# First modulation and projection by quarters of the features; two projection chunks as seven block products

## The chip, the cores and the metric

The kernel runs as one program on one core of a Trainium2 chip. The metric is the time of the whole program on the device in microseconds, the median of several runs. TensorE (PE) does matrix products and transposes into the eight banks of PSUM, VectorE (DVE), ScalarE (ACT) and GpSimd (POOL) do elementwise work, and SyncE (SP) issues nearly all transfers from memory in one queue.

## The reference, cut to what matters

All of it is float32, for 256 tokens of 1024 features. The part that is touched is the start of the first block:

```python
def first_block(x, c, ada_w, ada_b, ln1_g, ...):
    cond = jax.nn.silu(c)
    mod = (cond @ ada_w[l] + ada_b[l])[:, None, :]
    sh1, sc1, g1, sh2, sc2, g2 = jnp.split(mod, 6, axis=-1)
    h = rms_norm(x, ln1_g[l]) * (1.0 + sc1) + sh1
    x = x + g1 * hybrid_mixer(h, w_in[l], w_out[l], ...)   # starts with h @ w_in, 2840 columns
    h = rms_norm(x, ln2_g[l]) * (1.0 + sc2) + sh2
    return x + g2 * sparse_moe(h, ...)                      # 32 experts, top 4
```

The mixer cuts the 2840 columns of `h @ w_in` into queries, keys and values of two attention variants. One of them compresses its keys with a small network (`cmp_w1`, `cmp_w2`). A second block with 272 tokens follows.

## The kernel before, in words

Features lie on the 128 partitions, in eight chunks of 128. Every engine has a program of its own, written out in order, and waits on counting semaphores. The weights of the first block pass through a ring of four slots of 2 MB. The list `A_LOADS` gives their order, and `a_freed(n)` the semaphore value at which the load in the same slot, four places earlier in the list, has been used: SP waits for that before it issues load n+4, and everything behind it in the list waits too.

The head runs so. x is transposed on TensorE (L872), copied out and squared on ScalarE (L1753, L1763), summed over the features with a matrix of ones (L880), and its root and reciprocal taken (L1765, L2130). The first third of the modulation (shift and scale, 2048 columns) is a product of `cond` with four loads of 2 MB (`mod`): two halves of the rows for each of two halves of the features. One group of matmuls takes four column groups of TensorE's array at a time (L889). VectorE copies the result out, TensorE transposes it, and VectorE adds the bias and scales the chunks of h (L2106 to L2121).

The projection runs over six chunks of columns (five of 512, one of 280) and two halves of the tokens, twelve products v = 0 to 11. The first four are done in two halves of the features (L947 to L973), with the remaining modulation between them. Products 4 to 11 (L975, L1018) contract all eight feature chunks at once. In between, TensorE transposes keys and queries (L986 to L1006), and runs the compression network (L1008), whose weights are the load `cmp`.

The second third of the modulation is summed over the rows on VectorE, in four passes over four loads (`add_modulation`, L2146). A product with ones then finishes it (L913). The last third runs on TensorE in eight halves (L901): two before the attention scores, six among them. The scores start with `score(0)` (L1084, L1143). From there on, attention, output projection, experts and the second block follow. The second block already uses the form of seven products of quarter blocks (Strassen's, in Winograd's variant), and the change takes its tables `UP_PRODUCTS` and `UP_FREED` over. GpSimd is idle between building its constants at the start and the attention's scaling, apart from copies of keys (L714) and a memset.

Of the kernel before, what the change touches and what calls it, by code (L numbers as in the profile page):

```python
# [40 lines left out]
P = 128  # L41
# [124 lines left out]
FIRST_SUMS = (QKV_SETS + 1, QKV_SETS + 1 + 2 * UP_SETS)  # L166
# [8 lines left out]
def b_freed(n):  # L175
# [17 lines left out]
    return "chunk_done", first + 4 * (c + 1)  # L193

# [69 lines left out]
class Memory:  # L264


    def __init__(self, nc, ctx):
# [68 lines left out]
        early_all = a.at  # L336
        self.modacc = self.OT.rearrange("p c t -> p (c t)")
# [140 lines left out]
z_done in_first z_copied doubled heads_ssq heads_root heads_normed gates_ready  # L478
# [34 lines left out]
def program_sync(nc, sp, m, s, a):  # L513
# [5 lines left out]
    def source(kind, layer, c):  # L519
# [4 lines left out]
        if kind == "mod":  # L524
            src = a["ada_w"][0, D // 2 * (c % 2):D // 2 * (c % 2 + 1), :].rearrange("(k p) n -> p k n", p=P)
            at = 512 * (c // 2)
            return [(slice(0, P), 2048, 512, src[:, :, at + D * n:at + D * n + 512]) for n in range(2)]
        if kind == "in" and c < 2:
            src = a["w_in"][0, D // 2 * c:D // 2 * (c + 1), 0:D]
            return [(slice(0, P), 4096, D, src.rearrange("(k p) n -> p k n", p=P))]  # L530
# [49 lines left out]
    for n, load_of in enumerate(A_LOADS):  # L580
# [3 lines left out]
        if load_of == ("in", 0, 5):  # L584
# [6 lines left out]
        elif n == RING - 1:  # L591
# [77 lines left out]
def program_gpsimd(nc, pool, m, s, a):  # L669
# [45 lines left out]

    pool.wait_ge(s["doubled"], 3)
    for u in range(UNITS):
        if u == 8:
            pool.wait_ge(s["heads_normed"], 5)
            pool.wait_ge(s["mod_ready"], 3)  # L720
# [121 lines left out]
def program_tensor(nc, pe, m, s, a):  # L842
# [21 lines left out]

    pe.wait_ge(s["c_loaded"], 16)
    turn_params(bank(0), 0, C)
    pe.wait_ge(s["x_loaded"], 16)
# [15 lines left out]
    def first_modulation(part):  # L883

        h, rows = part // 2, part % 2
# [2139 lines left out]
```

## Time and profile before

| | us |
|---|---|
| median of 3 runs | 1790.54 (1788.81 to 1790.69) |
| the profiled execution | 1793.06, its span 1791.3 |
| TensorE busy in the span | 1720.4 |
| VectorE, ScalarE, GpSimd busy | 712.0, 264.5, 134.5 |
| first projection starts | 23.86 |
| first attention scores start | 125.69 |

A float32 product of 512 columns shows as two records of TensorE, so eight matmuls are sixteen records. The granted clock is 1.00 at full speed (2.4 GHz) and 0.50 at the lower level (1.2 GHz). A row of the chain of waits names what the end waited for at that time. A transfer in it means that nothing else could have gone on.

### The profile page before, as it was taken

To read this page: it belongs to the slowest core of one execution; us is meant where nothing else is said; L and a number is where in the kernel's file an instruction comes from. 1 tells how busy PE (TensorE), PEld (TensorE's weight loads), DVE (VectorE), ACT (ScalarE), POOL (GpSimd) and SP (SyncE) were. 2 spreads that over 40 slices of the span, in tenths; PEclk is the share of its full clock that TensorE was granted. 3 is DMA by queue.
4 is the path that set the end of the run, shared out by engine and by line. 5 is a ranking of instruction groups with operands and counts; after the bars stand their busy time and mean duration, and the time that the engine had idled before them with its cause. 6 is when DMAs were issued, how large, how long until landed. Compare 5 with 4: busy or idle time off the path is not lost.

```text
span 1791.3 us, 25208 instructions
## 1 busy us (share of the span) xinstructions
PE 1720.4 (96%) x10215; PEld 1058.6 (59%) x10216; DVE 712.0 (40%) x1295; ACT 264.5 (15%) x535; POOL 134.5 (8%) x188
## 2 busy tenths in 40 slices
PE   7999999999999999999999999999999999999998
PEld 4456643333333333333333333797999998899987
DVE  2555422122121121212212121666678545768743
ACT  1136211011010100101011010214111001511100
POOL 4006400000000000001000010200100000010000
PEclk9999999999999999999999999999999999999999
DMA  8988999969999999999999999751254443535440
GB/s 313 342 284 249 387 417 429 430 283 428 429 428 428 427 428 428 429 428 428 428 428 428 429 428 428 262 187 48 95 185 145 172 159 118 200 142 188 159 171 24
DMA packets 95507, 548.11 MB, mean 306 GB/s; under 512 B 6002, under 2 KB 9282, under 8 KB 68722
## 3 DMA queue, kind: packets, MB, share of 16 engines
q1 hardware_dynamic: 95298, 546.93, 75.9%
q8 instruction: 48, 0.79, 0.2%
q10 hardware_dynamic: 144, 0.26, 0.0%
q14 instruction: 17, 0.14, 0.0%
HBM read 546.12 MB, written 1.05 MB: 305 GB/s over the span
## 4 chain that ended last, share of the span: by engine, by line
PE 77%; DMA 20%; ACT 1%; issue 1%; POOL 0%; DVE 0%; SPq 0%; DVEq 0%; POOLq 0%; ACTq 0%
DMA ring<-in_exp_w 18%; PE ps L1322 18%; PE ps L1609 11%; PE ps L1353 8%; PE ps L1638 6%; PE ps L1679 5%; PE ps L1454 4%; PE ps L1380 3%; PE ps L981 2%; PE ps L1287 2%; PE ps L1274 2%; PE ps L954 2%; PE ps L1195 2%; PE ps L1708 2%; DMA ring<-in_w_in 1%; PE ps L1733 1%
## 5 line engine op out<-in xcount | busy, mean ns | idle before, releaser
L1322 PE MATMUL ps<-ring,sq 128*64 128x512 f32 x2112 | 464.4, 593 | 23.9 <-DMA ring<-in_exp_w 23.9
L1322 PEld LDWEIGHTS ps<-ring,sq 128*64 128x64 f32 x2112 | 146.9, 137 | 316.7 <-issue 264.3
L1353 PE MATMUL ps<-arena,sq 128*64 128x512 f32 x1056 | 233.9, 595 | 3.5
L2360 DVE TENSOR_SCALAR sq<-arena,rstd 128x64 f32<-128x64 f32 x68 | 19.5, 329 | 365.2 <-PE ps L1322 364.6
L1353 PEld LDWEIGHTS ps<-arena,sq 128*64 128x64 f32 x1056 | 75.3, 137 | 140.8 <-issue 140.5
L2433 DVE TENSOR_SCALAR hn<-ps 128x512 f32<-128x512 f32 x33 | 22.8, 691 | 318.4 <-PE ps L1322 318.4
L1860 ACT ACTIVATE sq<-hn 128x512 f32<-128x512 f32 x33 | 20.8, 629 | 527.8 <-DVE hn L2433 527.8
L1753 ACT ACTIVATE sq<-ps 128x512 f32<-128x512 f32 (+1 forms) x99 | 51.9, 524 | 308.7 <-PE ps L1353 212.2
L1609 PE MATMUL ps<-arena 128*128 128x136 f32 (+1 forms) x768 | 90.0, 277 | 0.0
L1609 PEld LDWEIGHTS ps<-arena 128*128 128x128 f32 x768 | 88.6, 191 | 0.0
L1753 ACT ACTIVATE arena<-ps 128x512 f32<-128x512 f32 (+4 forms) x69 | 33.8, 500 | 279.8 <-PE ps L1638 78.4
L2483 DVE TENSOR_TENSOR arena<-ring 128x1024 f32<-128x1024 f32 x37 | 45.7, 1234 | 65.2 <-PE ps L1638 33.5
L1287 PEld LDWEIGHTS ps<-sq 64*128 64x128 f32 x528 | 48.7, 186 | 32.7 <-issue 26.0
L1287 PE MATMUL ps<-sq 64*128 64x256 f32 x528 | 66.9, 390 | 0.8 <-ACT sq L1753 0.7
L798 POOL TENSOR_TENSOR sq<-sq 128x272 f32<-128x272 f32 (+1 forms) x28 | 28.6, 1022 | 497.4 <-ACT sq L1880 294.8
L1274 PE MATMUL ps<-arena,sq 128*64 128x512 f32 x272 | 64.1, 592 | 0.2 <-DVE arena L2362 0.2
L1638 PE MATMUL ps<-arena 128*128 128x136 f32 x512 | 61.9, 279 | 0.0
L782 POOL TENSOR_TENSOR arena<-arena 32x1 f32<-32x1 f32 x5 | 0.9, 183 | 808.9 <-PE ps L1322 808.9
L1609 PE MATMUL ps<-hn,ring 128*128 128x136 f32 (+1 forms) x512 | 60.9, 277 | 0.0
L1638 PEld LDWEIGHTS ps<-arena 128*128 128x128 f32 x512 | 60.5, 190 | 0.0
L1609 PEld LDWEIGHTS ps<-hn,ring 128*128 128x128 f32 x512 | 59.6, 191 | 0.1
L1679 PE MATMUL ps<-arena 128*128 128x256 f32 x256 | 57.9, 379 | 0.0
(437 smaller groups left out, 2254.0 us busy)
## 6 DMA issues: line engine op xcount, KB each, us to landing
ring<-in_exp_w SPq DMA_DIRECT2D x123, 2048.0 KB, 21.1
arena<-in_exp_w SPq DMA_DIRECT2D x68, 2048.0 KB, 19.4
ring<-in_mlp_w_up SPq DMA_DIRECT2D x16, 2048.0 KB, 7.5
ring<-in_mlp_w_down SPq DMA_DIRECT2D x16, 2048.0 KB, 7.8
ring<-in_ada_w SPq DMA_DIRECT2D x8, 2048.0 KB, 12.3
ring<-in_sb_w_qkv SPq DMA_DIRECT2D x6, 2048.0 KB, 14.7
ring<-in_w_in SPq DMA_DIRECT2D x5, 2048.0 KB, 12.3
ring<-in_ada_w SPq DMA_DIRECT2D x8, 1024.0 KB, 9.9
```

The lines of the kernel that those rows point to most:

```text
L954: last = mm(bank(v), m.hn[:, kk, META + P * t:META + P * t + P], wt[:, k, at:at + 512], start=(kk == 0), stop=(kk == C - 1))
L1274: last = mm(bank(0)[64 * h:64 * h + 64, :], m.sel[:, t, :], m.h2[:, t, 512 * h:512 * h + 512], start=(t == 0), stop=(t == 1))
L1287: return mm(m.token_sum(c), m.y[rows, P * (c % 4):P * (c % 4) + P], m.selz[rows, h, :], start=False, stop=stop, skip_group_check=True)
L1322: last = mm(bank(2 + part)[64 * h:64 * h + 64, :], lhs, w[:, k % 2, at:at + 512], start=False, stop=(k == C - 1))
L1353: last = mm(bank(3)[64 * h:64 * h + 64, :], m.aT[:, q, 64 * half:64 * half + 64], w[:, q, 512 * h:512 * h + 512], start=(half == 0 and q = ...
L1380: last = mm(bank(banks[q] if banks else b0 + q)[:, lo:TT], w[:, k, P * q:P * q + P], act[:, k, lo:TT], start=(n == 0), stop=(n == C - 1))
L1454: last = mm(bank(qkv_bank(n, j))[:, half * f:half * f + half], weights_of(weights, w, m.wsum[:, n % 2], k)[:, P * f:P * f + P], inputs_of( ...
L1609: last = mm(bank(set_bank(n, j))[:, half * f:half * f + half], weights_of(weights, w, m.wsum[:, n % 2], k)[:, P * f:P * f + P], inputs_of( ...
L1638: last = mm(bank(b)[:, half * f:half * f + half], weights_of(weights, w, m.wsum[:, n % 2], k)[:, P * f:P * f + P], hidden_of(tokens, 0, gr ...
L1679: last = mm(bank(b)[:, 0:256], hidden_of(tokens, 1, group, k), weights_of(weights, w, m.wsum[:, n % 2], k), start=(group == 0 and k == 0), ...
L1753: f(dst, src, ACT.Copy, scale=scale).then_inc(s[name], 1)
L2483: link(v.tensor_tensor(t1, w[:, 0, :, 1], w[:, 0, :, 0], ALU.subtract))
```

## The change

Order of loads: the modulation's first third comes as four quarters of the features (all rows, 2 MB each), and with each of them the matching quarter of the rows of `w_in` for the first three column chunks (1304 columns, 1.3 MB). Behind them come chunks 3, 4 and 5 of the projection and the second modulation group by turns. `cmp` goes ahead of that group's last load. The loads of the biases of the experts now stand behind `cmp` and not behind the last chunk.

Head: VectorE copies x out of PSUM, and ScalarE only squares it, with its table loaded ahead. The reciprocal is applied to quarters. Filler products of the identity with itself (`idle_turns`) stand at six places of TensorE's program. The first three column chunks (v = 0 to 5) run in quarters of the features, the next quarter's modulation between them.

Chunks 4 and 5 (1024 columns) become two sets of seven products, each of four matmuls with 256 columns, instead of two products of eight with 512 for each. GpSimd makes four sums of token blocks once and four sums of weight blocks for each set (128x1024). ScalarE copies each set's first product, and VectorE adds the others up (`z_put`). The products are spread over the same places among the transposes.

The second third's last load is used on TensorE, by eight matmuls more in `modulation_sum`, and VectorE has three passes in the place of four. This sum and its transposes move behind the products. Semaphore counts of later users are shifted. The diff, cut to its core:

```diff
-A_LOADS = ([("mod", 0, 0), ("mod", 0, 1), ("in", 0, 0), ("mod", 0, 2), ("mod", 0, 3)]
-           + [("in", 0, 1), ("in", 0, 2), ("ada", 1, 0), ("ada", 1, 1), ("in", 0, 3), ("ada", 1, 2), ("in", 0, 4),
-              ("ada", 1, 3), ("in", 0, 5), ("cmp", 0, 0)] + [("ada", 2, k) for k in range(4)] + [("wout", 0, h) for h in range(2)])
+QUARTERS = 4
+IN_FIRST = 1304
+A_LOADS = ([(kind, 0, q) for q in range(QUARTERS) for kind in ("mod", "inq")]
+           + [("in", 0, 3), ("ada", 1, 0), ("in", 0, 4), ("ada", 1, 1), ("in", 0, 5), ("ada", 1, 2), ("cmp", 0, 0),
+              ("ada", 1, 3)] + [("ada", 2, k) for k in range(4)] + [("wout", 0, h) for h in range(2)])
+Z_SETS, Z_DENSE = 2, QUARTERS - 1 + 8
+Z_BANK = (0, 1, 7, 2, 3)
 A_CMP, A_N = A_LOADS.index(("cmp", 0, 0)), len(A_LOADS)
 LATE_PARTS = (0, 1, 4, 7)
-MOD_BANK, MOD_TURN_BANK = (6, 7, 7), (5, 7, 7)
+MOD_BANK, MOD_TURN_BANK = (6, 1, 7), (5, 2, 7)
...
-    if (kind, c) == ("in", 0):
-        return "in_first", 1
+    if kind == "inq":
+        return "z_done", (1, 2, 3, 9)[c]
+    if kind == "in":
+        return "z_done", (Z_DENSE, Z_DENSE + 7, Z_DENSE + 14)[c - 3]
     if (kind, layer) == ("ada", 1):
-        return "mod_added", c + 1
-    return {"mod": ("mod_parts", c + 1), "ada": ("mod_parts", 4 * layer + c + 1), "in": ("z_done", 2 * (c + 1)),
+        return ("mod_added", c + 1) if c < 3 else ("mod_parts", 8)
+    return {"mod": ("mod_parts", c + 1), "ada": ("mod_parts", 4 * layer + c + 1),
...
+    pool.wait_ge(s["h_ready"], C)
+    x = [[m.hn[:, 4 * f:4 * f + 4, META + P * t:META + P * t + P] for f in range(2)] for t in range(2)]
+    s1, s2, s3, s4 = (m.xsum[:, i] for i in range(4))
+    g.tensor_tensor(s1, x[1][0], x[1][1], ALU.add).then_inc(s["h_summed"], 1)
+    pool.wait_ge(s["h_summed"], 1)
+    g.tensor_tensor(s2, s1, x[0][0], ALU.subtract).then_inc(s["h_summed"], 1)
+    g.tensor_tensor(s3, x[0][0], x[1][0], ALU.subtract).then_inc(s["h_summed"], 1)
+    pool.wait_ge(s["h_summed"], 2)
+    g.tensor_tensor(s4, x[0][1], s2, ALU.subtract).then_inc(s["h_summed"], 1)
+    for n in range(Z_SETS):
+        r, amount = A_AT[A_LOADS.index(("in", 0, 4 + n))]
+        pool.wait_ge(s.loaded[r], amount)
+        w = m.ring[:, r, :].rearrange("p (f k h n) -> p f k h n", f=2, k=4, h=2)
+        t1, t3, t4 = m.zsum[n]
+        t2 = w[:, 0, :, 1]
+        link(g.tensor_tensor(t1, w[:, 0, :, 1], w[:, 0, :, 0], ALU.subtract))
+        link(g.tensor_tensor(t3, w[:, 1, :, 1], w[:, 0, :, 1], ALU.subtract))
+        g.tensor_tensor(t2, w[:, 1, :, 1], t1, ALU.subtract).then_inc(s["w_differed"], 1)
+        pool.wait_ge(s["w_differed"], n + 1)
+        g.tensor_tensor(t4, t2, w[:, 1, :, 0], ALU.subtract).then_inc(s["w_summed"], 1)
...
+    idle_turns(2)
     pe.wait_ge(s["c_loaded"], 16)
     turn_params(bank(0), 0, C)
+    idle_turns(8)
...
+    def first_modulation(q):
+
+        w = a_slot(A_LOADS.index(("mod", 0, q))).rearrange("p (n k f) -> p n k f", n=2, f=256)
+        for k in range(C):
             for r in range(4):
-                last = mm(bank(MOD_BANK[0])[32 * r:32 * r + 32, 256 * h:256 * h + 256], m.condR[:, 4 * rows + k, :],
-                          w[:, r // 2, k, 256 * (r % 2):256 * (r % 2) + 256],
-                          start=(rows == 0 and k == 0), stop=(rows == 1 and k == 3))
+                last = mm(bank(MOD_BANK[0])[32 * r:32 * r + 32, P * q:P * q + P], m.condR[:, k, :],
+                          w[:, r // 2, k, P * (r % 2):P * (r % 2) + P], start=(k == 0), stop=(k == C - 1))
         last.then_inc(s["mod_parts"], 1)
...
-        pe.wait_ge(s["mod_added"], 4)
+        w = a_slot(A_LOADS.index(("ada", group, 3))).rearrange("p (k n) -> p k n", n=2048)
+        for kk in range(2):
+            for r in range(4):
+                mm(bank(MOD_BANK[group])[32 * r:32 * r + 32, :], m.condR[:, 6 + kk, :], w[:, kk, 512 * r:512 * r + 512],
+                   start=(kk == 0), stop=False)
+        pe.wait_ge(s["mod_added"], 3)
         for r in range(4):
             last = mm(bank(MOD_BANK[group])[32 * r:32 * r + 32, :], m.ones[:, 0:32], m.modacc[:, 512 * r:512 * r + 512],
-                      start=True, stop=True)
+                      start=False, stop=True)
         last.then_inc(s["mod_parts"], 4)
...
+    for q in range(QUARTERS - 1):
+        for v in range(4):
+            project_quarter(v, q)
+        first_modulation(q + 1)
+        project_quarter(4, q)
+        turn_first_modulation(q + 1)
+        project_quarter(5, q).then_inc(s["z_done"], 1)
+    for v in range(6):
+        project_quarter(v, QUARTERS - 1).then_inc(s["z_done"], 1)
...
+    def projected_set(n, products):
+
+        r = A_AT[A_LOADS.index(("in", 0, 4 + n))][0]
...
+            if j == 2:
+                pe.wait_ge(s["h_summed"], 4)
+                pe.wait_ge(s["w_differed"], n + 1)
+            if j == 5:
+                pe.wait_ge(s["w_summed"], n + 1)
...
+    projected_set(0, range(4))
+    pe.wait_ge(s["heads_normed"], 1)
+    pe.wait_ge(s["turned_dve"], 1)
+    turned_pairs(4, 0, 0)
+    projected_set(0, range(4, 7))
+    pe.wait_ge(s["turned_dve"], 2)
+    turned_pairs(5, 0, 2)
+    projected_set(1, range(3))
+    pe.wait_ge(s["heads_normed"], 3)
+    pe.wait_ge(s["turned_act"], 1)
+    turned_keys(4)
+    pe.wait_ge(s["consts_ready"], 2)
+    compressed_hidden()
+    projected_set(1, range(3, 5))
...
+    def set_product(n):
+        act.wait_ge(s["z_done"], Z_DENSE + 7 * n + 1)
+        if n:
+            act.wait_ge(s["z_added"], 7 * (n - 1) + 2)
+        copy(m.zpart[:, 0, :], bank(Z_BANK[7 * n % 5])[:, 0:256], "z_copied")
...
+    for b in range(4):
+        dve.wait_ge(s["x_turned"], b + 1)
+        v.tensor_copy(m.xT[:, 2 * b:2 * b + 2, META:TT], bank(1 + b).rearrange("p (c t) -> p c t", c=2)).then_inc(
+            s["x_placed"], 1)
```

TensorE (PE) from its first instruction, before. L889 is a group of the modulation, L954 the first projection products.

```order
L863 MATMUL ps<-ident,arena 128x8
L872 MATMUL ps<-ident,arena 128x128 x16
L880 MATMUL ps<-sq,ones 128x256 x8
L889 MATMUL ps<-ring,arena 32x256 x16
L863 MATMUL ps<-ident,arena 128x104
L889 MATMUL ps<-ring,arena 32x256 x16
L898 MATMUL ps<-ident,arena 128x128 x2
L954 MATMUL ps<-ring,hn 128x512 x8
L889 MATMUL ps<-ring,arena 32x256 x16
L954 MATMUL ps<-ring,hn 128x512 x4
L889 MATMUL ps<-ring,arena 32x256 x16
L954 MATMUL ps<-ring,hn 128x512 x2
```

And after, with L905 the filler, L932 a modulation group and L1000 the projection.

```order
L905 MATMUL ps<-ident 128x128 x2
L900 MATMUL ps<-ident,arena 128x8
L905 MATMUL ps<-ident 128x128 x8
L916 MATMUL ps<-ident,arena 128x128 x16
L924 MATMUL ps<-sq,ones 128x256 x8
L900 MATMUL ps<-ident,arena 128x104
L905 MATMUL ps<-ident 128x128 x4
L932 MATMUL ps<-ring,arena 32x128 x32
L905 MATMUL ps<-ident 128x128 x2
L938 MATMUL ps<-ident,arena 128x128
L905 MATMUL ps<-ident 128x128 x3
L1000 MATMUL ps<-ring,hn 128x512 x8
```

One modulation group stands ahead of the first projection product where there were two, and fillers stand around it; each group has 32 narrow matmuls in the place of 16.

TensorE from the chunk with number 4 on, before. L981 is the projection, L917 the modulation's sum, L1014 the compression network, L990, L924 and L1005 are transposes.

```order
L981 MATMUL ps<-ring,hn 128x512 x8
L990 MATMUL ps<-ident,arena 128x128 x4
L981 MATMUL ps<-ring,hn 128x512 x8
L917 MATMUL ps<-arena,ones 32x512 x4
L990 MATMUL ps<-ident,arena 128x128 x4
L981 MATMUL ps<-ring,hn 128x512 x8
L924 MATMUL ps<-ident,arena 128x128 x4
L1005 MATMUL ps<-ident,arena 128x128 x4
L1014 MATMUL ps<-ring,arena 64x128 x32
L981 MATMUL ps<-ring,hn 128x512 x4
L1047 MATMUL ps<-ident,arena 128x128
L990 MATMUL ps<-ident,arena 128x128 x4
```

And after, from the fifth product of the first set on. L1090 is a product, L1055 the compression network, L1031 and L1046 are transposes.

```order
L1090 MATMUL ps<-arena 128x256 x4
L1090 MATMUL ps<-arena,hn 128x256 x4
L1090 MATMUL ps<-ring,arena 128x256 x4
L1031 MATMUL ps<-ident,arena 128x128 x4
L1090 MATMUL ps<-ring,hn 128x256 x8
L1090 MATMUL ps<-ring,arena 128x256 x4
L1046 MATMUL ps<-ident,arena 128x128 x4
L1055 MATMUL ps<-ring,arena 64x128 x32
L1090 MATMUL ps<-sq,arena 128x256 x8
L1117 MATMUL ps<-ident,arena 128x128
L1031 MATMUL ps<-ident,arena 128x128 x4
L1090 MATMUL ps<-arena,hn 128x256 x4
```

Three products of the second set stand ahead of the compression network, and the modulation's sum has gone behind them all.

SP's queue from the load of the last projection chunk (`in_w_in 128x8x512`) on, before:

```order
L559 DMA ring<-in_w_in 128x8x512 [waits z_done]
L586 DMA arena<-in_exp_b 32x2048 x3
L588 DMA arena<-in_exp_b 32x1024
L559 DMA ring<-in_nsa_cmp_w 128x32x128 [waits mod_added]
L559 DMA ring<-in_ada_w 128x2x2048 [waits z_done]
L559 DMA ring<-in_ada_w 128x2x2048 [waits mod_added]
L559 DMA ring<-in_ada_w 128x2x2048 [waits z_done]
```

And after:

```order
L575 DMA ring<-in_w_in 128x8x512 [waits z_done]
L575 DMA ring<-in_ada_w 128x2x2048 [waits mod_added]
L575 DMA ring<-in_nsa_cmp_w 128x32x128 [waits z_done]
L602 DMA arena<-in_exp_b 32x2048 x3
L604 DMA arena<-in_exp_b 32x1024
L575 DMA ring<-in_ada_w 128x2x2048 [waits mod_added]
L575 DMA ring<-in_ada_w 128x2x2048 [waits z_done]
```

The load of the compression weights (`in_nsa_cmp_w`) waited for a pass of VectorE (`mod_added`) and now waits for a count of products (`z_done`, 18, the end of the first set). The first load of the last modulation group is the last row shown of the new order, and waits for `z_done` 25, the end of the second set. `mod_parts`, `mod_added` and `cmp_hidden` free the slots of the loads behind.

## Rows read from the trace of the kernel before

**Rows 1.** The page: busy time of each engine.
```profile
PE 1720.4 (96%) x10215; PEld 1058.6 (59%) x10216; DVE 712.0 (40%) x1295; ACT 264.5 (15%) x535; POOL 134.5 (8%) x188
```

**Rows 2.** Chain of waits, 0 to 230 us: start us, us, what (xcount).
```profile
23.86 8.72 PE ps L954 x16
32.58 1.86 PE ps L889 x32
...
58.44 9.33 DMA ring<-in_w_in
67.91 8.80 PE ps L981 x16
77.15 6.87 PE ps L981 x16
...
108.00 3.64 PE ps L1014 x64
...
119.64 1.46 PE ps L990 x12
121.09 1.85 PE ps L908 x16
...
123.72 1.97 PE ps L1075 x16
125.69 2.44 PE ps L1091 x16
...
176.83 3.46 PE ps L1195 x16
```

**Rows 3.** Timeline, head: start us, us, engine, line, tiles, shapes, count [idle before <-releaser].
```profile
6.79 3.54 PE L872 MATMUL ps<-ident,arena 128*128 128x128 f32 x16 [4.21 <-DMA arena<-in_x]
...
11.62 3.69 PE L880 MATMUL ps<-sq,ones 128*128 128x256 f32 x16 [1.30 <-ACT sq L1763]
...
15.93 1.75 DVE L2130 RECIPROCAL rstd<-root 128x256 f32<-128x256 f32 x1 [12.27 <-ACT root L1765]
...
17.84 1.93 PE L889 MATMUL ps<-ring,arena 128*32 128x256 f32 x32 [0.42 <-DMA ring<-in_ada_w]
...
21.26 2.17 DVE L2120 TENSOR_SCALAR hn<-hn,affine,modT 128x256 f32<-128x256 f32 x4
...
23.86 8.72 PE L954 MATMUL ps<-ring,hn 128*128 128x512 f32 x16 [3.04 <-DMA ring<-in_w_in]
```

**Rows 4.** Windows: engines' busy us, granted clock, DMA share, GB/s.
```profile
24.00:26.00 2.00, 2.00 (x3) 0.97 (x4) 0.56 (x1) 0.00 (x0) 0.00 (x0) 0.50 1.05 387
...
66.00:68.00 2.00, 0.09 (x1) 0.12 (x2) 1.53 (x7) 0.88 (x3) 0.00 (x0) 1.00 0.52 120
68.00:70.00 2.00, 2.00 (x3) 0.91 (x4) 1.05 (x4) 0.30 (x1) 0.00 (x0) 0.52 0.94 369
...
126.00:128.00 2.00, 2.00 (x16) 1.61 (x12) 1.93 (x10) 0.42 (x1) 0.00 (x0) 0.53 0.99 418
...
99.00:100.00 1.00, 1.00 (x12) 0.40 (x5) 0.20 (x1) 0.31 (x1) 0.00 (x0) 1.00 1.06 291
```

**Rows 5.** Transfers issued at 66.0 and at 86.74 us: KB each, us to landing.
```profile
ring<-in_ada_w SPq DMA_DIRECT2D x1, 2048.0 KB, 7.8
...
ring<-in_nsa_cmp_w SPq DMA_DIRECT2D x1, 0.5 KB, 17.6
```

**Rows 6.** Timeline: VectorE and GpSimd between 89 and 98 us, and late in the program.
```profile
89.11 3.90 DVE L2172 TENSOR_TENSOR arena<-ps,prm 64x120 f32<-64x120 f32 x16
93.04 4.74 DVE L2156 SCALAR_TENSOR_TENSOR arena<-ring,arena 128x2048 f32<-128x2048 f32 x2
...
1736.18 2.18 POOL L830 TENSOR_TENSOR arena<-arena 128x512 f32<-128x512 f32 x1 [0.40 <-DVE arena L2740]
...
1737.27 2.18 DVE L2485 TENSOR_TENSOR arena<-ring,arena 128x1024 f32<-128x1024 f32 x1
...
1783.24 1.27 POOL L830 TENSOR_TENSOR arena<-arena 128x512 f32<-128x512 f32 x1 [1.00 <-DVE arena L2740]
```

More of the change, by code:

```diff
@@ L524, in source @@
         if kind == "mod":
[L525 to L530, printed above, removed]
+            src = a["ada_w"][0].rearrange("(k p) n -> p k n", p=P)
+            at = 256 * c
+            return [(slice(0, P), 2048, 256, src[:, :, at + D * n:at + D * n + 256]) for n in range(2)]
+        if kind == "inq":
+            src = a["w_in"][0, 256 * c:256 * c + 256, 0:IN_FIRST]
+            return [(slice(0, P), 2 * IN_FIRST, IN_FIRST, src.rearrange("(k p) n -> p k n", p=P))]
         if kind == "in":
@@ L863, in turn_params, with idle_turns @@
         turn(out[:, 0:rows], m.params[0:rows, n, :], ident[0:rows, 0:rows]).then_inc(s["prm_turned"], 1)
+    def idle_turns(count):
+        for _ in range(count):
+            mm(bank(4)[:, 0:P], ident, ident, start=True, stop=True)
+    idle_turns(2)
     pe.wait_ge(s["c_loaded"], 16)
     turn_params(bank(0), 0, C)
+    idle_turns(8)
     pe.wait_ge(s["x_loaded"], 16)
@@ L1045, in program_tensor @@
-    project(11, range(4))
+    def projected_set(n, products):
+        r = A_AT[A_LOADS.index(("in", 0, 4 + n))][0]
+        w = a_slot(A_LOADS.index(("in", 0, 4 + n))).rearrange("p (f k h n) -> p f k h n", f=2, k=4, h=2)
+        for j in products:
+            (tokens, *tn), (weights, *wn) = UP_PRODUCTS[j]
+            g = 7 * n + j
+            if g < 5:
+                pe.wait_ge(s["z_copied"], (1, 2, 6, 7, 8)[g])
+            else:
+                before, of = (g - 5) // 7, (g - 5) % 7
+                if of == 0:
+                    pe.wait_ge(s["z_copied"], 8 + before + 1)
+                else:
+                    pe.wait_ge(s["z_added"], 7 * before + UP_FREED[of])
+            if j == 2:
[3 more added lines that the diff above has]
+                pe.wait_ge(s["w_summed"], n + 1)
+            for k in range(4):
+                if tokens == "sum":
+                    x = m.xsum[:, tn[0], k, :]
+                else:
+                    x = m.hn[:, 4 * tn[1] + k, META + P * tn[0]:META + P * tn[0] + P]
+                if weights == "weights":
+                    y = w[:, wn[0], k, wn[1], :]
+                elif wn[0] == 1:
+                    y = w[:, 0, k, 1, :]
+                else:
+                    y = m.zsum[n][{0: 0, 2: 1, 3: 2}[wn[0]]][:, k, :]
+                last = mm(bank(Z_BANK[g % 5])[:, 0:256], x, y, start=(k == 0), stop=(k == 3))
+            last.then_inc(s["z_done"], 1)
@@ new lines, in program_tensor @@
+    pe.wait_ge(s["z_copied"], 3)
+    project(6, range(C))
+    pe.wait_ge(s["cond_ready"], 2)
+    pe.wait_ge(s["z_copied"], 5)
+    pe.wait_ge(s["doubled"], 3)
+    turned_twice(4, 0)
+    pe.wait_ge(s["z_copied"], 4)
+    project(7, range(C))
+    turned_twice(5, 1)
+    projected_set(0, range(4))
[5 more added lines that the diff above has]
+    turned_pairs(5, 0, 2)
@@ L2190, in program_vector @@
         last.then_inc(s["heads_normed"], 1)
-        for part in {0: (0, 1), 2: (2,)}.get(c, ()):
-            add_modulation(part)
-        if c == 3:
+        if c == 2:
+            add_modulation(0)
+            add_modulation(1)
+        elif c == 3:
             blocks(0, 4, 0)
             blocks(1, 5, 1)
-            add_modulation(3)
-            modulation_rows(1)
+            for number in range(1, 8):
+                z_put(0, number)
         elif c == 4:
@@ L2202, in program_vector @@
                             ALU.mult).then_inc(s["turned_dve"], 1)
-            modulation(1)
+    z_put(1, 1)
+    z_put(1, 2)
+    add_modulation(2)
     dve.wait_ge(s["cmp_hidden"], 1)
@@ L2227, in program_vector @@
     v.tensor_copy(m.kcn[0:64, 0, :], m.kcn[0:64, 1, :]).then_inc(s["cmp_dve"], 1)
+    modulation(1)
     dve.wait_ge(s["cmp_kT_done"], 1)
```

281 lines of the change are left out of this document (143 added, 138 removed).

## The prediction

> **What bounds the kernel now.** I read the page first: TensorE is busy for 96% of the span, so only the stretches where it is idle or slow, and its own work, can move the end [rows 1]. The change ends in the first 130 us, so I then read the chain of waits from 0 to 230 us [rows 2], the head's timeline [rows 3], the clock by short windows [rows 4], and the transfers [rows 5]. They show this. The first projection starts at 23.86 us, after 3.04 us idle for its weights, and sixteen records then take 8.72 us where sixteen equal ones take 6.87 later: 1.85 us lost to a granted clock of 0.50, the 1.2 GHz level. The same happens once more: the chain leaves L981 for a transfer, TensorE has 0.09 us of work between 66 and 68, the clock is 0.52 afterwards, and sixteen records take 8.80 us, 1.93 too many. The next 55 us are dense. The attention scores start at 125.69 us (L1091). Behind that point the order of work is the same in both kernels apart from semaphore counts, so I forecast how that instant moves. The profiled execution took 1793.06 us beside a span of 1791.3, and the median of the runs is 1790.54, 2.5 below it: I sum against the former and take the difference off the median.
>
> **Part 1, the start.** Before, x lands at 6.79 and sixteen transposes take 3.54 us, 0.22 each; later ones take 0.12 [rows 2, 3]. With filler products running before x arrives I take the later price: done at 8.7. VectorE copies bank by bank while ScalarE squares, so the sums (3.69 us) end at about 12.3. Root 0.5, reciprocal 1.75 and a quarter's norm 0.7 lead to 15.3. TensorE meanwhile computes the first quarter of the modulation, its 2.1 MB being in by about 13, until 16.0. From the end of that group before (19.77) to the first scaled chunk (21.8) it was 2.0 us, so the projection starts at 18.2: −5.7 us. It needs 4.5 MB (x is 1.05, a modulation quarter 2.1, the first quarter of the weights 1.3, all by their shapes) where 7.3 MB had to land before. There is no idle 3 us ahead, so the slow 1.85 us go as well. Together −7.5.
>
> **Part 2, the modulation in quarters.** Before, two groups of 32 records ran after the start, 1.86 us each. Now three do, each of 64 records of half the width. With time by columns a group stays at 1.86, with time by records it is 3.7; the 64 narrow records of L1014 took 3.64, but they fill only two column groups at a time. I take 2.4, nearer to the lower end, since four stationary loads overlap in a row of the timeline: 3×2.4−3.7+0.1 for a transpose more = +3.6 (bounds +2.0 and +7.5).
>
> **Part 3, the stall at 66 us.** The fourth chunk is now requested behind the third modulation quarter, at about 40 us, and needed at 61: the idle 1.95 and the slow 1.93 go, −3.9.
>
> **Part 4, seven products.** Chunks five and six took four groups of 6.87, 27.5 us. Fourteen products of four 256-column matmuls at 3.46/8 each make 24.2: −3.3. The sum of the modulation now has eight matmuls more, which L908 did in 1.85: +1.85, and VectorE has two passes of 2.37 less.
>
> **Part 5, GpSimd's sums.** They start when the third and fourth block are copied, about 61 us: four token sums of 512 elements, then four weight sums of 1024 for each set. Alone, 512 elements took 1.27 us [rows 6]; twice that for 1024, less a fixed part, is 2.35. Alone, all that the third product needs is ready at 61+5+7=73, ahead of TensorE's 79. But VectorE is at the modulation's passes (2.37 each) and the norms in that stretch. Rows 6 show what then happens: an addition on GpSimd took 2.18 instead of 1.27 behind a VectorE addition, and the VectorE addition that came next took 2.18 as well. They take turns. Taking turns from 61 to 86 us, with the second modulation block in at 69, gives the third product at 81.5 and the blocks of keys (L2172, 3.90 us for both) so late that the transposes behind the fourth product, due at 82.4, start at 87. Whoever waits for them waits on TensorE, in order. I charge +4.0; bounds 0 (GpSimd stays ahead) and +8 (each step blocked, in the second set too). The page "SBUF — State Buffer" of the Trainium skill, section "Who interferes with whom", says that a VectorE instruction with two SBUF inputs and a GpSimd instruction that reads SBUF exclude each other for a whole instruction; the trace agrees, 2.18 against 1.27. By a rule of shared bandwidth both would lose a little at a time.
>
> **Part 6, the order of loads.** Two loads now hang on late events. The compression weights reuse the slot of the fifth chunk and may start only after its seventh product; they are needed 6.0 us later (transposes 0.4, three products 5.2, transposes 0.4). Before, they were requested at 86.74 and took 17.6 us behind others. Their 2.1 MB at the 291 GB/s of that stretch need 7.2 us, with 2.7 around them (an isolated load of that size took 7.8 where its bytes need 4.9): 9.9 in all. TensorE is idle for 3.9 us, and after 3.0 and 1.95 us idle the clock fell both times: +1.9. Then the first block of the third modulation group waits for all fourteen products, takes 7.8 us, and is needed after 0.4+2.9+1.3=4.6 us: +3.3 idle. The slow clock after it costs less, +1.5, since little dense work follows. Together +10.6.
>
> Sum: −7.5+3.6−3.9−3.3+1.85+4.0+10.6 = +5.4 us at 125.69. Before, the clock fell to 0.53 at 126 us anyway, and part of that loss (about 1.4 us by the row) may now coincide with the one charged: −0.8. So +4.6: 1797.7 for an execution like the profiled one, **1795.1 us** for the median.
>
> **Rivals.** (a) The late loads don't bind and the start gives all it can: faster. For it: the start and the stall are worth 11.4 us by rows. Against: both loads wait for products that end only a few microseconds before TensorE asks. Its point is what the six and four and a half microseconds of cover hide: with no slow clock after either wait (−3.4), GpSimd ahead (−4.0) and groups at 1.86 (−1.6) the sum is −4.4, or 1786. Chance 0.17. (b) GpSimd stays ahead and all else is as charged: +4.6−4.0, 1791.1, no difference. It decides on how the turns fall; chance 0.25. (c) Records, not columns, set the modulation groups (+3.9) and the turns cost the full 8 (+4.0, halved as the wait for the compression weights hides the second set): +10.5, 1801. Chance 0.10. (d) The start doesn't come forward as the name says: pieces of 1 KB in the modulation quarters are slower than 2 KB ones, and the first quarter lands at 15 or 16 us. That adds 2 to 3: 1797.5 to 1798. Chance 0.10. My forecast has the remaining 0.38.
>
> **From these to the numbers.** A measurement of this kernel can tell about 0.2% (3.6 us) from no change. The forecast's own range is 1791 to 1799, with three tenths of it inside the 0.2%. Slower: 0.26+0.10+0.10, and some of (b): 0.49. Same: 0.11+0.20 and the edge of (a): 0.33. Faster: 0.18. The range reaches from case (a) at 1786 to 1799.5, which leaves about 0.1 on either side.
>
> **What would show it.** In the new profile: the first projection record at 18.2 us with clock 1.0 (right) or above 20 (wrong); modulation groups of 64 records in 2.4 us; no wait at the fourth chunk; GpSimd additions of 1024 elements at 2.3 us alone and above 3 beside VectorE; TensorE idle some 4 us until the compression weights and 3 us until the next modulation load, each with a lower clock behind; the scores at 130 to 131 us. If the scores start below 126 us, the late loads were dearer in my sum than on the chip, and the forecast is wrong. If the difference sits behind the scores, its ground is.

## The result, and the profile after

| | before | changed |
|---|---|---|
| median, us | 1789.9 (1788.8 to 1790.7, 4 runs) | 1810.3 (1808.3 to 1812.1, 4 runs) |
| ratio to before | | 1.0114, 95% interval 1.0101 to 1.0127 |
| profiled execution, its span | 1793.06, 1791.3 | 1808.31, 1806.5 |
| first projection starts | 23.86 | 18.20 |
| attention scores start | 125.69 | 140.76 |

The change makes the kernel 20 us slower; 5 were forecast, with 1799.5 as the upper end. The page of the changed kernel, first line of its busy times (engine, busy us, share, instructions): TensorE is busy for 5.6 us more than in [rows 1], work at a slow clock among it, while the span is 15.2 longer; so most of the loss is waiting.

```profile
PE 1726.0 (96%) x10445; PEld 1078.2 (60%) x10446; DVE 730.8 (40%) x1319; ACT 260.7 (14%) x529; POOL 165.2 (9%) x200
```

The chain of waits of the changed kernel, 15 to 160 us (start us, us, what), its longer pieces. It answers to [rows 2]:

```profile
18.20 7.10 PE ps L1000 x16
...
68.20 3.31 DVE arena L2239
71.53 4.33 DVE arena L2241
...
84.60 3.25 DVE arena L2305
...
109.00 4.40 issue
113.39 5.00 PE ps L1055 x64
...
126.07 7.54 DMA ring<-in_ada_w
...
133.75 3.28 PE ps L945 x16
...
140.76 2.80 PE ps L1165 x16
```

The start is as forecast, at 18.2. At 56 us the chain leaves TensorE, which it had not done between 68 and 123 us before, and comes back only at 95.34: 39 us through VectorE's queue, the last 27 of them from the modulation passes (L2239) on. Further down are the two waits that were forecast: 4.40 us (the chain calls it issue; the matmuls behind it are those of the compression network, which need the load `cmp`), and the transfer that the third modulation group waits for. The piece behind each is at the slow clock: 5.00 us where 3.64 had been, 3.28 where 1.85 had been.

The timeline of the changed kernel around the long wait, engine by engine (start us, us, engine, line, tiles, shapes, count, and in brackets the idle time before it and its releaser):

```profile
68.12 3.37 DVE L2239 TENSOR_SCALAR arena<-ring,arena 128x2048 f32<-128x2048 f32 x1
71.53 13.04 DVE L2241 SCALAR_TENSOR_TENSOR arena<-ring,arena 128x2048 f32<-128x2048 f32 x3
84.60 3.24 DVE L2305 TENSOR_TENSOR arena<-arena 128x1024 f32<-128x1024 f32 x1
87.88 1.22 DVE L2306 TENSOR_REDUCE arena<-arena 128x16 f32<-128x1024 f32 x1
...
89.75 3.58 DVE L2312 TENSOR_TENSOR arena<-arena 128x512 f32<-128x512 f32 x2
93.26 3.90 DVE L2257 TENSOR_TENSOR arena<-ps,prm 64x120 f32<-64x120 f32 x16
...
73.78 4.28 POOL L749 TENSOR_TENSOR ring<-ring,arena 128x1024 f32<-128x1024 f32 x1
78.13 4.28 POOL L751 TENSOR_TENSOR arena<-ring 128x1024 f32<-128x1024 f32 x1
...
95.34 1.09 PE L1031 MATMUL ps<-ident,arena 128*128 128x128 f32 x4 [12.05 <-DVE arena L2257]
```

TensorE has no work for 12.05 us. L1031 are the transposes of the queries, and they wait for the block sums of L2257, at the end of VectorE's queue. Above them stands why VectorE is late. A modulation pass takes 4.33 us (13.04 for three) and not 2.37 [rows 6], the first, one-input pass 3.37 where it took 1.28 in the trace of before, the norm's square 3.24 for 1.23, and its two products (L2312) 3.58 together for 1.29. GpSimd's additions of 1024 elements stand at 4.28 beside them. The reduction of L2306 keeps its time. The rows of before:

```profile
56.39 1.28 DVE L2154 TENSOR_SCALAR arena<-ring,arena 128x2048 f32<-128x2048 f32 x1
...
84.76 1.23 DVE L2181 TENSOR_TENSOR arena<-arena 128x1024 f32<-128x1024 f32 x1 [6.16 <-ACT arena L1753]
```

The clock of the changed kernel by windows (the granted clock is the number before the DMA share), one inside the wait and one behind it:

```profile
88.00:90.00 2.00, 0.00 (x0) 0.00 (x0) 1.59 (x3) 0.58 (x2) 2.00 (x1) 0.50 0.00 0
...
96.00:98.00 2.00, 2.00 (x8) 1.64 (x7) 1.91 (x8) 0.69 (x1) 0.00 (x0) 0.50 0.00 0
```

Term by term, at the instant the scores start, the two first profiles give:

| term | forecast | measured |
|---|---|---|
| start, and the slow clock in the head | -7.5 | -7.3 |
| modulation in quarters, hops between groups | +3.6 | +3.0 |
| the stall at 66 and its slow clock | -3.9 | -3.9 |
| fourteen products for four groups | -3.3 | -3.3 |
| eight matmuls more in the sum | +1.85 | +1.85 |
| GpSimd's sums beside VectorE | +4.0 | +14.0 (12.05 idle, 0.65 and 1.33 of slow clock) |
| compression weights | +5.8 | +5.8 (4.40 and 1.36) |
| third group's first load | +4.8 | +4.9 (3.16, 1.43 and 0.33) |
| coincidence with the clock at 126 | -0.8 | 0 |
| sum | +4.6 | +15.1 (the instants: 15.07) |

One term is wrong, by 10 us. The coincidence would show behind that instant: the next 40 records took 5.85 us before and 5.51 after in this pair of executions, and 5.84 in both kernels in the second pair (experiment 10).

### The profile page after: what moved, and what is told of

The parts are those of the page before. It is cut to its first block, busy times and chain, and to the rows that moved or that the text cites. A ratio compares the mean times of both kernels' runs of the same rounds, so it can differ in the third digit from the quotient of the medians.

```text
span 1806.5 us, 25713 instructions
## 1 busy us (share of the span) xinstructions
PE 1726.0 (96%) x10445; PEld 1078.2 (60%) x10446; DVE 730.8 (40%) x1319; ACT 260.7 (14%) x529; POOL 165.2 (9%) x200
## 3 DMA queue, kind: packets, MB, share of 16 engines
HBM read 546.12 MB, written 1.05 MB: 303 GB/s over the span
## 4 chain that ended last, share of the span: by engine, by line
PE 75%; DMA 19%; DVE 2%; ACT 1%; issue 1%; POOL 0%; SPq 0%; DVEq 0%; POOLq 0%; ACTq 0%
DMA ring<-in_exp_w 18%; PE ps L1396 18%; PE ps L1683 11%; PE ps L1427 8%; PE ps L1712 6%; PE ps L1753 5%; PE ps L1528 4%; PE ps L1454 3%; PE ps L1361 2%; PE ps L1348 2%; PE ps L1000 2%; PE ps L1269 2%; PE ps L1782 2%; PE ps L1090 1%; PE ps L1807 1%
## 5 line engine op out<-in xcount | busy, mean ns | idle before, releaser
L1396 PE MATMUL ps<-ring,sq 128*64 128x512 f32 x2112 | 464.4, 593 | 24.4 <-DMA ring<-in_exp_w 24.4
L1396 PEld LDWEIGHTS ps<-ring,sq 128*64 128x64 f32 x2112 | 146.9, 137 | 317.1 <-issue 264.7
L2616 DVE TENSOR_TENSOR arena<-ring 128x1024 f32<-128x1024 f32 x37 | 45.7, 1235 | 65.2 <-PE ps L1712 33.5
L1827 ACT ACTIVATE arena<-ps 128x256 f32<-128x256 f32 (+4 forms) x67 | 32.0, 489 | 261.9 <-PE ps L1712 78.4
```

The costliest lines, as they stand in the source:

```text
L1396: last = mm(bank(2 + part)[64 * h:64 * h + 64, :], lhs, w[:, k % 2, at:at + 512], start=False, stop=(k == C - 1))
L1827: f(dst, src, ACT.Copy, scale=scale).then_inc(s[name], 1)
L2616: link(v.tensor_tensor(t1, w[:, 0, :, 1], w[:, 0, :, 0], ALU.subtract))
```

## The experiments

Theory A: VectorE and GpSimd exclude each other on SBUF for whole instructions, and all that VectorE loses this way lies on the path, since nothing in its queue is spare. Theory B: VectorE's queue is in a bad order (it starts 5 us later, and four passes stand ahead of the norm), GpSimd or not. Theory C: the two share a bandwidth.

**1. GpSimd's sums nearly left out** (`e1_tiny`). The products take unsummed blocks.

```diff
-    x = [[m.hn[:, 4 * f:4 * f + 4, META + P * t:META + P * t + P] for f in range(2)] for t in range(2)]
+    x = [[m.hn[:, 4 * f:4 * f + 4, META + P * t:META + P * t + 8] for f in range(2)] for t in range(2)]
-        t1, t3, t4 = m.zsum[n]
+        t1, t3, t4 = (t[:, :, 0:8] for t in m.zsum[n])
```

> The changed kernel with GpSimd's twelve block sums cut to 8 columns each; the products that used sums take unsummed blocks in their place (same shapes and count), so chunks 4 and 5 of the projection come out wrong, the routing may differ, and one expert pass more or less moves the total by some 14 us. It is therefore read at the instant the attention scores start (140.76 in the changed kernel, 125.69 before). Theory A, VectorE and GpSimd exclude each other by whole instructions: the modulation passes fall from 4.33 back to 2.35, TensorE's 12.05 us of idle at 83.3 falls under 1 and the slow clock behind it (2.2 us) goes, so the scores start at 126 to 127. Theory B, the order of VectorE's queue (it starts 5 us later, passes ahead of the norm): the idle time stays at 6 us or more and the scores start at 134 or later. The waits for the compression weights (4.4) and for the third group (3.2) stay in both.

Measured: 1781.02, ratio 0.9952 (0.9938 to 0.9967), with one expert pass less (2048 records of L1396 for 2112). From the scores to the end it is 14.9 us shorter than the changed kernel (1650.8 for 1665.7), which I put down to that pass. Its timeline up to the scores:

```profile
67.10 2.35 DVE L2241 SCALAR_TENSOR_TENSOR arena<-ring,arena 128x2048 f32<-128x2048 f32 x1
70.99 4.74 DVE L2241 SCALAR_TENSOR_TENSOR arena<-ring,arena 128x2048 f32<-128x2048 f32 x2 [1.53 <-DMA ring<-in_ada_w]
76.93 1.23 DVE L2305 TENSOR_TENSOR arena<-arena 128x1024 f32<-128x1024 f32 x1 [1.20 <-ACT arena L1827]
...
81.28 3.90 DVE L2257 TENSOR_TENSOR arena<-ps,prm 64x120 f32<-64x120 f32 x16
...
83.38 0.61 PE L1031 MATMUL ps<-ident,arena 128*128 128x128 f32 x4
```

and its chain:

```profile
127.70 2.86 PE ps L1165 x16
```

The passes are back at 2.35, no idle time stands before L1031, and the scores start at 127.70, 13.1 us earlier (126 to 127 was expected; the wait for the compression weights and the slow clock behind it cost 0.6 more here). Theory B is out. Ahead of the norm VectorE has 2.7 us to spare, the two waits in its rows. Behind it almost nothing is: the first half of the blocks ends at 83.23 (81.28 and half of 3.90), and TensorE takes up the transposes at 83.38. What VectorE loses from the norm on, TensorE loses in full. With the 14.9 us added the time would be 1795.9, an estimate.

**2. GpSimd's sums in quarters** (`e2_split`), each instruction as four.

```diff
-    g.tensor_tensor(s1, x[1][0], x[1][1], ALU.add).then_inc(s["h_summed"], 1)
+    for k in range(4):
+        last = g.tensor_tensor(s1[:, k], x[1][0][:, k], x[1][1][:, k], ALU.add)
+    last.then_inc(s["h_summed"], 1)
...
```

> The changed kernel with each of GpSimd's sums issued as four instructions of a quarter each. Theory A (turns by whole instructions): a modulation pass waits for one short addition only, 2.35 plus 0.4 to 0.7, so 2.8 to 3.1 instead of 4.33, while each short addition waits for a whole pass: GpSimd's first weight sums end far later, the third product waits for them, and the scores start between 138 and 145. Theory C (both share a bandwidth): passes stay at 4.3, nothing moves by more than 1 us, and the time stays at 1810.

Measured: 1806.18, ratio 1.0091 (1.0078 to 1.0104); scores at 137.5. Its timeline:

```profile
67.96 7.35 DVE L2257 SCALAR_TENSOR_TENSOR arena<-ring,arena 128x2048 f32<-128x2048 f32 x3
...
62.67 1.79 POOL L736 TENSOR_TENSOR arena<-hn 128x128 f32<-128x128 f32 x4
...
66.34 6.82 POOL L743 TENSOR_TENSOR arena<-hn 128x128 f32<-128x128 f32 x4
...
87.26 3.53 PE L1106 MATMUL ps<-ring,arena 128*128 128x256 f32 x8 [7.33 <-POOL ring L762]
```

Three passes take 7.35, 2.45 each. GpSimd's quarters of 128 elements had taken 1.79 for four; now four take 6.82, and the single ones that meet a pass take 2.50 each. The total work is the same and the loser has changed: GpSimd gets in once for each pass, with a quarter of the work. TensorE now waits 7.33 us for GpSimd in front of the third product. Theory C would have left both as they were. The passes came out below my 2.8 to 3.1, so a pass hardly waits for a short addition.

**3. The additions alone, in the kernel before** (`e4_before_gps`), with results that nobody uses.

```diff
+    for i in range(12):
+        ...
+        link(g.tensor_tensor(out, x, y, ALU.add))
```

> The kernel before with twelve additions on GpSimd that nobody uses (four of 512 elements and eight of 1024, reading h, from 61 us on). It is the suspected cost alone. Theory A: the modulation passes that meet them take 4.3 instead of 2.35 and the norm at 84.8 (1.23) about 3.2; VectorE has several microseconds of slack there, so the transposes due at 91.3 come 2 to 5 us late: 1792 to 1796 (ratio 1.001 to 1.004). Theory B or C: no VectorE instruction over 1.3 times its time of before, the total unchanged.

Measured: 1795.80, ratio 1.0035 (1.0023 to 1.0047). Its timeline:

```profile
72.58 8.48 DVE L2164 SCALAR_TENSOR_TENSOR arena<-ring,arena 128x2048 f32<-128x2048 f32 x2 [0.23 <-DMA ring<-in_ada_w]
81.09 3.26 DVE L2189 TENSOR_TENSOR arena<-arena 128x1024 f32<-128x1024 f32 x1
...
91.86 1.09 PE L998 MATMUL ps<-ident,arena 128*128 128x128 f32 x4 [4.96 <-DVE arena L2180]
```

The same lengths in another kernel: 4.24 for a pass, 3.26 for the square, as expected. The transposes that had no idle time before wait 4.96 us for L2180, the blocks.

**4. Fills in their place** (`e12_memset`): GpSimd is as busy, writes more (four fills for each long addition), and reads nothing.

```diff
-        link(g.tensor_tensor(out, x, y, ALU.add))
+        for _ in range(4 if i >= 4 else 2):
+            link(g.memset(out, 0.0))
```

> The kernel before with fills in the place of the twelve unused additions on GpSimd, in the same stretch and for about the same 34 us: GpSimd writes and reads nothing. If what excludes is GpSimd's reading, the modulation passes stay at 2.35 and the norm at 1.23, and the time at 1789 to 1791. If GpSimd's being busy or its writing is enough, the passes take over 3 us and the time is 1794 to 1797, as with additions.

Measured: 1790.36, ratio 0.9998 (0.9989 to 1.0008). Its timeline:

```profile
71.97 4.74 DVE L2165 SCALAR_TENSOR_TENSOR arena<-ring,arena 128x2048 f32<-128x2048 f32 x2 [4.06 <-DMA ring<-in_ada_w]
83.62 1.23 DVE L2190 TENSOR_TENSOR arena<-arena 128x1024 f32<-128x1024 f32 x1 [6.91 <-ACT arena L1762]
...
59.48 36.87 POOL L723 MEMSET arena<- 128x512 f32 x40
```

Forty fills fill GpSimd for 36.87 us, and the passes (2.37) and the square (1.23) do not notice. So for these two-input instructions it is GpSimd's reading of SBUF that excludes, not its being busy and not its writing. No scaling of VectorE met a fill, so for that one the question stays open.

**5. The passes behind the first set** (`e5_late_passes`).

```diff
-            add_modulation(0)
-            add_modulation(1)
...
             for number in range(1, 8):
                 z_put(0, number)
+            add_modulation(0)
+            add_modulation(1)
```

> The changed kernel with the first two modulation loads' passes (four VectorE instructions) moved behind the first set's sums; GpSimd as it is. Theory A: the norm at 76.5 takes 3.2 + 1.2 + 3.6 beside GpSimd and ends near 85.5, the blocks' first half 2 us later, so TensorE's idle at 83.3 falls from 12.05 to about 4. The passes free slots later, so the compression weights' load is asked for after about 98 instead of 103 while they are needed at 101: an idle 7 us in the place of 4.4. Scores at 134 to 137, time 1802 to 1807. If TensorE still waits 9 us or more at 83, the order of the passes was not what held it.

Measured: 1807.06, ratio 1.0094 (1.0078 to 1.0109). TensorE's rows with idle time:

```profile
84.08 0.63 PE L1031 MATMUL ps<-ident,arena 128*128 128x128 f32 x4 [0.69 <-DVE arena L2257]
...
111.71 5.69 PE L1055 MATMUL ps<-ring,arena 128*64 128x128 f32 x64 [15.76 <-issue]
```

The wait at the queries falls to 0.69 where 4 was expected, since GpSimd had then finished the first set by 77.8 and met only the square. But the load of the compression weights comes behind the passes in SP's queue, and 15.76 us are lost there where 7 was expected; the scores start at 139.44 and not at 134 to 137. Order alone moves the loss on: what is left of it, 3 us, is within the overlap of the intervals of this variant and the changed kernel.

**6. Quarters in the head, dense chunks** (`e3_dense`).

```diff
-    projected_set(0, range(4))
+    project(8, range(C))
...
-    projected_set(0, range(4, 7))
+    project(9, range(C))
```

> The changed kernel with the quarters of the head kept and chunks 4 and 5 as four dense products of 6.87 us, no sums on GpSimd, the same order of loads. Theory A: no exclusion, VectorE ready at 83; from 76.22 the work of before (41.23 us to the scores) plus 1.85 for the eight matmuls, about 3 for the wait for the compression weights with its slow clock and 4.9 for the third group's: scores at 127.2, time 1790 to 1793 (ratio to before 1.000 to 1.0015). Theory B: a wait of 5 us or more stays at the first transposes of the queries, 1796 or more.

Measured: 1795.79, ratio 1.0033 (1.0021 to 1.0045), 3 us above what was expected; the scores start at 129.20 and not at 127.2, 0.3 of it from a start at 18.50 and 1.5 from the two waits. Both waits for loads, by the timeline:

```profile
101.42 5.38 PE L1034 MATMUL ps<-ring,arena 128*64 128x128 f32 x64 [2.76 <-issue]
...
122.17 3.53 PE L924 MATMUL ps<-ring,arena 128*32 128x512 f32 x16 [3.21 <-DMA ring<-in_ada_w]
```

Without the seven products 14.5 of the 20 us are gone. The medians agree with the estimate of experiment 1 (1795.9), while the scores start 1.5 us later here than there. So even with sums that cost nothing the products, 3.3 us by their rows, bring only 1.5 us at the scores, the waits for the two loads taking 1.8 back, and nothing that the medians show. The two waits cost 2.76 + 1.74 and 3.21 + 1.68, 9.4 in all, as in the forecast's way of reckoning.

**7. The loads in another order** (`e6_dense_loads` on the dense variant, `e8_loads` on the changed kernel). Two neighbouring pairs change places:

```diff
-           + [("in", 0, 3), ("ada", 1, 0), ("in", 0, 4), ("ada", 1, 1), ("in", 0, 5), ("ada", 1, 2), ("cmp", 0, 0),
+           + [("in", 0, 3), ("ada", 1, 0), ("ada", 1, 1), ("in", 0, 4), ("ada", 1, 2), ("in", 0, 5), ("cmp", 0, 0),
```

> The quarters of the head with dense chunks 4 and 5, and the loads in another order: chunk 4, the second group's third load and chunk 5 each one place later, so that the compression weights reuse the slot of the second modulation load, and the third group's first load that of a modulation load too, not of chunk 5. If the two waits cost what the trace of the dense variant shows (idle 2.76 plus 1.74 of slow clock, idle 3.2 plus 1.7), this gives 9 us back: 1786 to 1788, ratio to before 0.998 to 0.999. If other transfers only move into the gap, 1790 or more.

By the edit the second group's third load comes one place earlier, not later.

Measured: 1786.49, ratio 0.9981 (0.9972 to 0.9990), the fastest version here and faster than both kernels, by 3 us and by 24. Its chain of waits:

```profile
98.31 3.64 PE ps L1034 x64
...
114.11 1.85 PE ps L924 x16
```

The compression network (L1034) follows without a wait at 3.64 us, and the third group (L924) at 1.85. This is the order of loads alone.

On the changed kernel the same two pairs change places, and the loads of the experts' biases move too, behind the second group's last load:

```diff
-        if load_of == ("cmp", 0, 0):
+        if load_of == ("ada", 1, 3):
```

> The changed kernel, sums on GpSimd as they are, with the reordered loads. The idle 12 us at 83.3 stay; the 4.4 + 1.4 us at the compression weights and the 3.2 + 1.4 + 0.4 at the third group go: scores at 130 to 131, time 1799 to 1801. If the stall and the late loads hide one another, less than 5 us comes back.

Measured: 1790.44, ratio 1.0002 (0.9992 to 1.0011): 20 us back where 10 were expected, by the two edits together. Its timeline:

```profile
68.38 1.27 DVE L2239 TENSOR_SCALAR arena<-ring,arena 128x2048 f32<-128x2048 f32 x1
69.69 11.07 DVE L2241 SCALAR_TENSOR_TENSOR arena<-ring,arena 128x2048 f32<-128x2048 f32 x3
...
70.85 3.39 POOL L747 TENSOR_TENSOR arena<-ring 128x1024 f32<-128x1024 f32 x1 [2.55 <-DMA ring<-in_w_in]
...
83.10 3.52 PE L1090 MATMUL ps<-ring,arena 128*128 128x256 f32 x8 [3.01 <-POOL ring L749]
...
89.39 0.63 PE L1031 MATMUL ps<-ident,arena 128*128 128x128 f32 x4 [1.05 <-DVE arena L2257]
```

Chunk 4 is asked for at 62.06 and not at 52.29, and takes 8.7 us where it took 12.9 beside another load, so it lands at 70.8 and not at 65.2, and GpSimd's weight sums start at 70.85 and not at 68.01. VectorE's first pass is then through in 1.27, the norm starts at 80.79 and not at 84.60, its two products take 1.44 together and not 3.58, and the queries wait 1.05 and not 12.05; the third product waits 3.01 for GpSimd, with slow clock behind it (3.52 for 1.73). So the collision is a matter of where two queues meet, and I had not seen that the order of loads sets that too.

**8. The fourth pass back on VectorE** (`e9_pass4`, on the dense variant with the new order).

```diff
-        for kk in range(2):
-            for r in range(4):
-                mm(bank(MOD_BANK[group])[32 * r:32 * r + 32, :], m.condR[:, 6 + kk, :], w[:, kk, 512 * r:512 * r + 512],
-                   start=(kk == 0), stop=False)
-        pe.wait_ge(s["mod_added"], 3)
+        pe.wait_ge(s["mod_added"], 4)
...
+    add_modulation(3)
     dve.wait_ge(s["cmp_kv_done"], 1)
```

> The dense variant with the reordered loads (1786.5), and the second third's fourth load summed on VectorE again (two passes of 2.37, behind the copy of the hidden layer) and not by eight matmuls on TensorE. VectorE idles from 101 to 112 there, so it should be free: -1.85 on TensorE, less up to 0.8 of wait for the last pass, so 1784.5 to 1786.5. If the load lands too late for VectorE, or the second transposes wait for VectorE, 1787 or more.

Measured: 1786.51, ratio 0.9983 (0.9974 to 0.9992), the same as without it, at the edge of what was expected (1784.5 to 1786.5). The chain:

```profile
93.90 12.75 DMA ring<-in_ada_w
106.68 2.36 DVE arena L2217
109.07 2.36 DVE arena L2217
```

The load lands at 106.65, and the two passes end at 111.43. In the version without them TensorE had its eight matmuls done at 111.79. The 1.85 us of work became a wait of the same length.

**9. Without the fillers** (`e7_no_fill`).

```diff
-        for _ in range(count):
-            mm(bank(4)[:, 0:P], ident, ident, start=True, stop=True)
+        return
```

> The changed kernel without the filler products. If they buy the clock of the head: the sixteen transposes of x take 3.5 instead of 1.9, the first sixteen projection records 8.7 instead of 7.1, first projection at 19 to 20; together +3 to +4 us, 1813 to 1815. If the transfers alone set the start: within 1 us of 1810.

Measured: 1811.92, ratio 1.0120 (1.0105 to 1.0136), which overlaps that of the changed kernel. Its timeline:

```profile
6.64 3.68 PE L915 MATMUL ps<-ident,arena 128*128 128x128 f32 x16 [3.92 <-DMA arena<-in_x]
...
19.15 7.10 PE L999 MATMUL ps<-ring,hn 128*128 128x512 f32 x16 [1.28 <-DVE hn L2199]
```

The transposes of x take 3.68 (1.91 with fillers), the projection starts 0.95 us later, and its records take 7.10 all the same. The fillers buy a microsecond at the start, and nothing that is clear of noise in the total. My 3 to 4 took a slow clock at the first projection for certain, and the next experiment shows that it isn't.

**10. Both kernels once more** (`before_again`, `after_again`), for a second profile of each.

> The kernel before once more, for a second profiled execution. The first took 1793.06 where the median of its runs is 1789.6. If the first sixteen projection records' slow clock (8.72 us) belongs to that execution alone, they take about 7.1 here, the projection starts near 23 and the scores near 123; if it belongs to the kernel, all is as in the first within 0.5 us.

Measured: 1792.01. Its timeline:

```profile
11.32 5.68 PE L880 MATMUL ps<-sq,ones 128*128 128x256 f32 x16 [1.30 <-ACT sq L1763]
...
23.61 7.10 PE L954 MATMUL ps<-ring,hn 128*128 128x512 f32 x16 [1.59 <-DVE hn L2120]
```

The slow clock is there in this execution too, only elsewhere: the sums of the squares take 5.68 (3.69 in [rows 3]), and the projection's first records 7.10 (8.72 there). The scores start at 124.28, 1.4 us earlier.

> The changed kernel once more, for a second profiled execution (the first took 1808.31, the median is 1810.3). The idle at the first transposes of the queries was 12.05 us; if the turns of VectorE and GpSimd fall otherwise from run to run, it differs by 1 us or more here; if not, the 2 us come from the head or from behind the scores.

Measured: 1809.72. The wait at the queries is 12.05 us again, so the turns fall alike. The difference lies behind the waits, in its chain:

```profile
108.53 4.64 issue
113.17 6.33 PE ps L1055 x64
...
141.86 2.26 PE ps L1165 x16
```

6.33 us for the compression network where the first execution took 5.00.

## Why the prediction was wrong

- **The start** was right (18.20), the clock with it, with one reservation: the slow clock stood at the first projection in one execution of before and in the sums in the other. The quarters as groups of 64 records took 1.88, below my 2.4; that is +2.0 by the forecast's sum, and the other 1.0 of the +3.0 are short waits and 280-column records around them (1.14 for the first four). The term came out near because two errors largely cancel. Rival (d), a late start, fell with it.
- **The stall at 66 us, the seven products, the sum's matmuls** were right to 0.1 us. The waits for the two loads were right in place and in their sums (5.8 and 4.9). At the compression weights there is luck in it: 3.9 idle and 1.9 of slow clock were forecast, 4.40 and 1.36 measured, and 4.64 and 2.69 in the second execution. Experiment 7 shows that the waits were needless: the same loads one place apart do not bind.
- **The step that failed is part 5, the term for GpSimd's sums beside VectorE.** The mechanism was right, the size was not: I charged +4.0 with a bound of 8, and it is 14.0. The prediction put the third product at 81.5 and the first transposes at 87; the product followed the second without a wait, and the transposes came at 95.34. What came late was VectorE, not GpSimd. Experiment 1 against the first profile says what I left out. Each of the four passes loses 2 us, the one-input pass too, where I had reckoned with turns of some 1 us from the one pair in [rows 6]. They also start 2.3 us later, at 68.12 and not at 65.79, since the norms of the smaller chunks meet the token sums; and the 2.7 us of waits ahead of the norm take that much off. So the norm starts at 84.60 and not at 76.93, 7.7 later. Then the second set's sums meet the norm: its square loses 2.0, its two products 2.3 together. That is 12.0, with 0.15 us of slack against it, and 2.0 of slow clock came on top. A bound for such a collision is worked out as full alternation: for every instruction of the one engine, one whole instruction of the other, as long as both have work. Seven instructions of VectorE (four passes, the square, two products) against sums of 2.35 us give some 16 us as an estimate of the bound, twice what I took.
- **Rival (b)**, that GpSimd stays ahead at no cost, is refuted by the same rows, and with it (a). Rival (c) was right on the turns (8, and still too low) and wrong on the groups.
- **The rest of the miss** is the step from the profiled execution to the median. I took 2.5 off, since the profile of before stood above its median. The two executions profiled of the changed kernel stand 2.0 and 0.6 below theirs. Runs of before alone spread from 1787.4 to 1794.0, and its profiles lay at 1793.06 and 1792.01. Between the second pair the scores differ by 17.6 us, between the medians the times differ by 20.4. Some 3 us of this are in no profile that I have. The granted clock tells something of them: its mean over a run was 0.996 in five runs of before, which took 1792.8 to 1794.0, and 0.999 in nineteen, which took 1787.4 to 1790.6, while the two profiled ones stand at 0.996 and 0.997. So the rows of before carry more slow clock than most of its runs. The stall at 66 us, which the forecast took off whole, is one place where it may lie: in the trace of experiment 3, whose program is that of before up to 60 us, it was 0.28 us idle and the sixteen records behind it took 7.10. In which stretch the median run is faster is not shown.

## What to carry to other kernels

Before work that reads SBUF goes to an idle GpSimd, look at what VectorE does at that moment with two inputs from SBUF, or a long scaling of one: with instructions of like length, each of the one waited for most of one of the other here, so as a bound charge one full instruction of the other for each, as long as both have work, and ask who waits for VectorE. Where it can't be moved, the engine that issues the shorter instructions loses (one experiment here), so the engine that TensorE waits for should issue the longer ones; fills cost two-input instructions nothing. And when products of a chunk free a ring slot, check what load hangs on it and how soon it is needed: one place in the order of loads was worth 9 us here, and, with the bias loads moved too, 20 where it also moved the collision. Last, before a stall is counted as gain, see in a second profile whether it is there each time.

## What the runs showed of the hardware

- Exclusion is by whole instructions and follows reading: two-input VectorE passes 2.37 to 4.33 beside GpSimd additions (2.35 to 4.28), the one-input scaling of 2048 elements 1.28 to 3.37, the reduction 1.22 beside additions as without them, and two-input instructions lose nothing beside fills (experiment 4). The Trainium skill, "SBUF — State Buffer", section "Who interferes with whom", says that a GpSimd instruction that only writes does not contend with two-input ones, and that scalings can take both port pairs while reductions never do: experiments 1 to 4 agree, with the lengths just given. It says further that the order of issue decides who blocks whom; in a stream of both, with neither out of work, GpSimd's short additions got in once for each pass (experiment 2: 2.50 us each beside a pass of 2.45, some 0.45 alone).
- While TensorE waited those 12 us the granted clock went to 0.50, the 1.2 GHz level, and it was still there at 96 to 98 us, with the engine at work again. What a wait costs in clock is not fixed: behind the 4.40 us at the compression weights it was 1.36 us in one execution of the changed kernel, and 2.69 behind 4.64 in the other; behind the 15.76 us of experiment 5 it was 2.05 (5.69 for 3.64).
